# First adaptive-norm modulation summed on TensorE instead of VectorE, with the first norm and its first transposes issued in the same stage

## The reference, cut to what matters

```python
cond = jax.nn.silu(c)                                     # c: 2048 values
mod = (cond @ ada_w[l] + ada_b[l])[:, None, :]            # ada_w: 2048 x 12288
sh1, sc1, g1, sh2, sc2, g2 = jnp.split(mod, 6, axis=-1)
h = rms_norm(x, norm_mix[l]) * (1.0 + sc1) + sh1
x = x + g1 * hybrid_mixer(h, w_in[l], ...)                # begins with h @ w_in
```

## Time and profile before

| | |
|---|---|
| time, median of 3 executions | 4131.59 us (4130.81 to 4135.14) |
| profiled execution, its own time | 4132.34 us |
| its span in the trace | 4130.6 us |
| granted clock of TensorE, mean | 0.945 of full |
| busy: PE, DVE, ACT | 3661.5, 2459.1, 1249.8 us |
| end of the last DVE sum, start of the first matmul of `project_in` | 132.9 us, 160.45 us |

### The profile page before, as it was taken

One profiled execution on the slowest core, in us unless ns is written; L12 is line 12 of the kernel. 1 busy time (PEld: TensorE's weight loads), 2 busy tenths in 40 slices (PEclk: granted clock), 3 DMA queues, 4 the chain that ended last, 5 costly groups with the idle time before them and its releaser, 6 DMA issues. The chain is left out here.

```text
span 4130.6 us, 47822 instructions
## 1 busy us (share of the span) xinstructions
PE 3661.5 (89%) x19719; PEld 2918.5 (71%) x19719; DVE 2459.1 (60%) x3050; ACT 1249.8 (30%) x1316; POOL 253.3 (6%) x413
## 2 busy tenths in 40 slices
PE   2699868999999999999999799777978998799798
PEld 1575547799999999888888678376854775444576
DVE  7665658589777754555555454755445444694464
ACT  1223223334444444333333343212312101100233
POOL 1011101000100000000000000020000211000000
PEclk9999869999999999999999899798988999899899
DMA  7875327455766676766666452203643111443563
GB/s 268 305 261 188 117 78 296 151 204 196 260 247 251 248 255 213 251 237 242 245 244 236 159 219 91 87 6 124 228 139 133 32 37 57 133 152 117 182 251 133
DMA packets 246294, 750.73 MB, mean 182 GB/s; under 512 B 31264, under 2 KB 42612, under 8 KB 210368
## 3 DMA queue, kind: packets, MB, share of 16 engines
q1 hardware_dynamic: 217008, 645.44, 44.5%
q0 software_dynamic: 29072, 102.25, 7.1%
HBM read 692.29 MB, written 54.75 MB: 181 GB/s over the span
## 5 line engine op out<-in xcount | busy, mean ns | idle before, releaser
L2076 DVE TENSOR_TENSOR expert_w_low<-expert_w,expert_w_high 128x2048 fp32r<-128x2048 f32 x256 | 586.5, 2291 | 556.3 <-ACT expert_w_high L2368 555.8
L2368 ACT ACTIVATE expert_w_high<-expert_w 128x2048 fp32r<-128x2048 f32 x256 | 489.4, 1912 | 431.6 <-PE bank L2357 410.6
L289 DVE TENSOR_TENSOR weights_low<-weights,weights_high 128x1024 fp32r<-128x1024 f32 (+2 forms) x328 | 387.2, 1183 | 354.9 <-ACT weights_high L272 351.7
L2298 PE MATMUL bank<-h_high,expert_w_high 128*128 128x256 f32 x2048 | 583.5, 285 | 9.2 <-DVE expert_w_low L2076 8.2
L2299 PE MATMUL bank<-h_low,expert_w_high 128*128 128x256 f32 x2048 | 580.2, 283 | 0.0
L2300 PE MATMUL bank<-h_high,expert_w_low 128*128 128x256 f32 x2048 | 580.2, 283 | 0.0
L272 ACT ACTIVATE weights_high<-weights 128x1024 fp32r<-128x1024 f32 (+2 forms) x328 | 335.9, 1026 | 559.2 <-PE bank L317 462.4
L2298 PEld LDWEIGHTS bank<-h_high,expert_w_high 128*128 128x128 f32 x2048 | 393.8, 192 | 10.1 <-DVE expert_w_low L2076 8.8
L2355 PE MATMUL bank<-expert_w_high,gated_acts_high 128*128 128x512 f32 x1024 | 398.3, 389 | 0.0
L2356 PE MATMUL bank<-expert_w_low,gated_acts_high 128*128 128x512 f32 x1024 | 398.3, 389 | 0.0
L2357 PE MATMUL bank<-expert_w_high,gated_acts_low 128*128 128x512 f32 x1024 | 398.3, 389 | 0.0
(11 more groups left out here) (661 smaller groups left out, 5694.6 us busy)
## 6 DMA issues: line engine op xcount, KB each, us to landing
expert_w<-in_peer_u_dram SPq DMA_DIRECT2D x128, 1024.0 KB, 5.9
expert_w<-in_peer_v_dram SPq DMA_DIRECT2D x128, 1024.0 KB, 4.9
weights<-in_w_in_dram SPq DMA_DIRECT2D x84, 1024.0 KB, 9.7
ada_ring<-in_ada_w_dram SPq DMA_DIRECT2D x64, 512.0 KB, 5.1
weights<-in_w_out_dram SPq DMA_DIRECT2D x32, 1024.0 KB, 13.6
s_gates_w<-in_w_in_dram SPq DMA_DIRECT2D x64, 512.0 KB, 3.4
s_in_w<-in_w_in_dram SPq DMA_DIRECT2D x48, 512.0 KB, 4.1
weights<-in_w_branch_dram SPq DMA_DIRECT2D x48, 512.0 KB, 5.8
```

The costliest lines, as they stand in the source:

```text
L289: dve.tensor_tensor(self.low[:, u % self.UNITS_HELD, :, 0:n], self.buf[b][:, k:k + self.UNIT, 0:n], self.high[:, u % self.UNITS_HELD, :, 0 ...
L2076: dve.tensor_tensor(wl[:, n % RING, :], w_sb[:, n % RING, :], wh[:, n % RING, :], ALU.subtract).then_inc(wl_ready, 1)
L2298: pe.matmul(o, uh[:, b, k, :], acts.h[:, k, :], start=(k == 0), stop=False)
L2368: act.activation(wh[:, n % RING, :], w_sb[:, n % RING, :], ACT.Copy).then_inc(wh_ready, 1)
```

## The change

The sum over `ada_w` moves from DVE to PE. `cond_spots` holds, for each block k and each of eight chunks j of 512 columns, a stationary operand of 128 rows by 8 columns that is zero but for column j, which is `cond[:, k]`. A matmul with it and half a piece as the moving operand adds chunk j's sums to row j of one PSUM bank; all 128 of them (16 blocks, 8 chunks) accumulate in the same bank of 8 x 512. DVE copies it, four small transposes make columns of it, and DVE adds the bias vector. The accumulator, its clearing (L431), the 64 additions of L459 and the 32 matmuls of L489 are gone.

DVE takes the vector columns and fills `cond_spots` before it builds the masks. PE makes the bias table after block 3 (`if k == KD // 4`). The first norm's `source` is now made ahead of the stage: ACT and DVE run `head_act` and `head_dve` in it, and PE runs `turn_first`, the first 16 transposes, after block 13. `headed = True` takes the heads out of `project_in`. SP's loop is written out. The core of the diff:

```diff
+        spots = m.sb(ctx, "cond_spots", [P, KD, SUMS, SUMS])
+        sums = m.sb(ctx, "mod_sums", [SUMS, CHUNK])
...
-                with sp.Fori(0, KD) as k:
+                for k in range(KD):
                     for b in range(4):
-                        sp.wait_ge(piece_used[b], k)
-                        sp.dma_start(ring[:, b, :], io["ada_w"][0, bass.ds(k * P, P), b * PIECE:(b + 1) * PIECE])\
+                        if k:
+                            sp.wait_ge(piece_used[b], k)
+                        sp.dma_start(ring[:, b, :], io["ada_w"][0, k * P:(k + 1) * P, b * PIECE:(b + 1) * PIECE])\
                           .then_inc(piece_loaded[b], 16)
...
+                V(dve.memset(spots[:, :, :, :], 0.0))
+                for g in range(3):
+                    bank = m.to_dve.get(dve)
+                    m.to_dve.free(dve.tensor_copy(st.vec.cols[:, g, :], bank[:, 0:P]))
+                dve.engine_nop()
+                dve.drain().then_inc(cols_ready, 1)
+                dve.wait_ge(cond_ready, 1)
+                dve.tensor_copy(view(spots[:, 0, 0, 0:1], [[SUMS * SUMS, KD], [SUMS + 1, SUMS]]),
+                                spread(cond[:, :], SUMS)).then_inc(spots_ready, 1)
...
                 bias_dve(dve, V)
-
-                dve.wait_ge(cond_ready, 1)
-                with dve.Fori(0, KD) as k:
-                    for b in range(4):
-                        dve.wait_ge(piece_loaded[b], 16 * (k + 1))
-                        part = acc[:, b * PIECE:(b + 1) * PIECE]
-                        dve.scalar_tensor_tensor(out=part, in0=ring[:, b, :], scalar=cond[:, bass.ds(k, 1)],
-                                                 in1=part, op0=ALU.mult, op1=ALU.add).then_inc(piece_used[b], 1)
-                        dve.wait_ge(piece_used[b], k + 1)
-                dve.drain().then_inc(acc_ready, 1)
+                source.head_dve(dve)
+
                 bank = m.to_dve.get(dve)
+                m.to_dve.free(dve.tensor_copy(sums[:, :], bank[0:SUMS, :]))
+                dve.drain().then_inc(sums_ready, 1)
...
                 bias_act(act)
+                source.head_act(act)
...
-                bias_pe(pe)
-
-                pe.wait_ge(acc_ready, 1)
-                pe.wait_ge(ones_ready, 1)
+                pe.wait_ge(spots_ready, 1)
+                total = m.to_dve.take(pe)
+                for k in range(KD):
+                    if k == KD // 4:
+                        bias_pe(pe)
+                    if k == KD - 2:
+
+                        m.to_act.take_all(pe)
+                        source.turn_first(pe)
+                    for b in range(4):
+                        pe.wait_ge(piece_loaded[b], 16 * (k + 1))
+                        for half in range(2):
+                            j = 2 * b + half
+                            mm = pe.matmul(total[0:SUMS, :], spots[:, k, j, :], ring[:, b, half * CHUNK:(half + 1) * CHUNK],
+                                           start=(k == 0 and j == 0), stop=(k == KD - 1 and j == SUMS - 1))
+                        if k < KD - 1:
+                            mm.then_inc(piece_used[b], 1)
+                m.to_dve.put(mm)
+                pe.wait_ge(sums_ready, 1)
                 bank = m.to_dve.take(pe)
-                for j in range(NM // P):
-                    mm = pe.matmul(bank[:, j:j + 1], acc[:, j * P:(j + 1) * P], ones[:, :], start=True, stop=True)
+                for q in range(CHUNK // P):
+                    mm = pe.transpose(bank[:, q * SUMS:(q + 1) * SUMS], sums[:, q * P:(q + 1) * P], st.ident[0:SUMS, 0:SUMS])
                 m.to_dve.put(mm)
```

More of the change, by code:

```diff
@@ L261, in split_high @@
         b, turn = self.chunk["act"] % 2, self.chunk["act"] // 2
-        if source:
+        if source and not source.headed:
             source.head_act(act)
@@ L363, in turn_to_columns, with stage_modulation @@
         ring.put(mm)
-def stage_modulation(nc, m, io, st):
+def stage_modulation(nc, m, io, st, source):
     NM = 2 * D
     PIECE = NM // 4
+    SUMS = NM // CHUNK
     with ExitStack() as ctx:
@@ L445, in _ @@
                     V(dve.tensor_tensor(st.level[:, lv, :], tmp[:, :], st.strict[:, :], ALU.mult))
-                for g in range(3):
-                    bank = m.to_dve.get(dve)
-                    m.to_dve.free(dve.tensor_copy(st.vec.cols[:, g, :], bank[:, 0:P]))
-                dve.engine_nop()
-                dve.drain().then_inc(cols_ready, 1)
-                bias_dve(dve, V)
-                dve.wait_ge(cond_ready, 1)
-                with dve.Fori(0, KD) as k:
-                    for b in range(4):
-                        dve.wait_ge(piece_loaded[b], 16 * (k + 1))
-                        part = acc[:, b * PIECE:(b + 1) * PIECE]
-                        dve.scalar_tensor_tensor(out=part, in0=ring[:, b, :], scalar=cond[:, bass.ds(k, 1)],
-                                                 in1=part, op0=ALU.mult, op1=ALU.add).then_inc(piece_used[b], 1)
-                        dve.wait_ge(piece_used[b], k + 1)
-                dve.drain().then_inc(acc_ready, 1)
-                bank = m.to_dve.get(dve)
-                m.to_dve.free(dve.tensor_tensor(st.mod_cols[:, 0:NM // P], bank[:, 0:NM // P],
-                                                st.vec.col("ada_b", 0, NM // P), ALU.add))
+                bias_dve(dve, V)
+                source.head_dve(dve)
+                bank = m.to_dve.get(dve)
+                m.to_dve.free(dve.tensor_copy(sums[:, :], bank[0:SUMS, :]))
+                dve.drain().then_inc(sums_ready, 1)
+                bank = m.to_dve.get(dve)
+                parts = CHUNK // P
+                m.to_dve.free(dve.tensor_tensor(view(st.mod_cols[:, 0:1], [[1, parts], [parts, SUMS]]),
+                                                view(bank[:, 0:1], [[SUMS, parts], [1, SUMS]]),
+                                                view(st.vec.col("ada_b", 0), [[1, parts], [parts, SUMS]]), ALU.add))
                 dve.drain().then_inc(mod_cols_ready, 1)
@@ L610 @@
     TURNED_AHEAD = 4
+    headed = False
     def __init__(self, m, st, name, dst, kt, k0=0):
@@ L646, in columns @@
         if unit == max(self.unit0 - 1, 0):
-            self.head_pe(pe)
-            while self.n_turn < min(self.TURNED_AHEAD, self.pairs):
-                self.turn_next(pe)
+            self.turn_first(pe)
         if p >= 0:
@@ L656, in head_pe, with turn_first @@
         pass
+    def turn_first(self, pe):
+        self.head_pe(pe)
+        while self.n_turn < min(self.TURNED_AHEAD, self.pairs):
+            self.turn_next(pe)
     def turn_next(self, pe):
@@ L972, in project_in @@
         m.weights.split_memory(ctx)
-        source = NormedColumns(m, ctx, st, "norm1", st.x, D, acts, lambda j: st.gain1[:, j:j + 1],
-                               lambda j: st.mod_cols[:, j:j + 1], proj[:, :, 0:D], lambda tt: proj[:, tt, 0:D],
-                               x_sem=(m.sem("x_loaded"), 32), keep=st.whole)
         mod = ModulationParts(m, io, st, ctx, "mod_mid", (2,))
@@ L3851, in whole_program @@
             m.weights.memory(c1)
-            stage_modulation(nc, m, io, st)
             proj = m.sb(c1, "projection_rows", [P, TT, N_IN])
+            source = NormedColumns(m, c1, st, "norm1", st.x, D, None, lambda j: st.gain1[:, j:j + 1],
+                                   lambda j: st.mod_cols[:, j:j + 1], proj[:, :, 0:D], lambda tt: proj[:, tt, 0:D],
+                                   x_sem=(m.sem("x_loaded"), 32), keep=st.whole)
+            source.headed = True
+            stage_modulation(nc, m, io, st, source)
             with ExitStack() as c2:
                 h1 = Split(m, c2, "h1", KD)
-                project_in(nc, m, io, st, h1, proj)
+                source.dst = h1
+                project_in(nc, m, io, st, h1, proj, source)
             rows = m.sb(c1, "mixer_rows", [P, TT, HALF])
```

8 lines of the change are left out of this document (3 added, 5 removed).

## The result

| | before | changed |
|---|---|---|
| time, median of 20 runs each | 4134.06 us (4128.98 to 4141.03) | 4141.96 us (4132.44 to 4147.11) |
| ratio to before, 95% interval | | 1.0017 (1.0010 to 1.0024) |
| profiled execution, own time and span | 4132.34, 4130.6 us | 4144.02, 4142.3 us |
| first matmul of the projection in it | 160.45 us | 166.22 us |
| busy: PE, DVE | 3661.5, 2459.1 us | 3765.0, 2375.3 us |

The change costs 7 us (4 to 10 by the interval), inside the 0.2% that the prediction called no change. DVE is relieved of 84 us and PE is given 103 more, and neither number is the 7.

What follows compares the result with a forecast made beforehand. The ring's round paced the old sums, PE the new. 14.2 + 110.1 + 2 + 5 + 23 + 2.4 + 2.5 + 5.5 = 164.7 us at the first matmul against 160.45, so 4136 us; range 4122 to 4150.

Steps and rivals of the forecast that it cites:

- Rival A: The forecast itself for the whole kernel: 4127 to 4149 us, its low end with the bias table at the higher clock; chance 0.66.
- Steps 3 and 4: During the sums on PE: 2 us for transfers under them; 5 us (2 to 8) for two cold starts of PE's clock.
- Step 1: Start of the stage: the first piece lands and PE's sums start at 14.2 us, bounds 12 to 16.
- Step 2: The sums on PE: 256 records at the higher clock, 0.43 us each, 110.1 us; at the lower clock 220.
- Rival B: PE never gets the higher clock in this stage: 4246 us; a partial fall costs 20 to 60 us more; chance 0.18.
- Step 5: Bias table in PE's line between two runs of sums: first five us at the higher clock, rest low, 23 us.
- rival C: Bias table also at the higher clock, 13.8 us for 23, no second cold start: 4124 to 4125 us; chance 0.09.
- Steps 6 to 8: After the bias table, turns 2.4 us; after the sums, tail 2.5; from gain to the projection's first matmul, head 5.5.
- Step 9: Transfers after the stage: next loads shift by 24 to 28 us against 25 of slack; cost 0, up to 5 us.
- rival D: Late weights hold up the projection's first or second chunk by 5 to 10 us: 4141 to 4146 us; chance 0.07.
- one to one: From the projection's first matmul (160.45 us before) to the end: a shift there carries to the kernel's end in full.
- the ring's round: DVE's sums before: 1.285 us use plus 5.1 landing plus issue, 6.7, over four buffers is the 1.675 us per piece.

Runs made afterwards that it cites:

- experiment 7: The changed kernel with bias table operands of 128 rows and six buffers for the pieces: 4128.77 us, ratio to the kernel before 0.9985.
- experiment 9: Against the kernel before: DVE sums 48 of 64 pieces, PE 16; bias table spread between pieces with 128 rows, early norm, seven buffers: 4094.64 us, ratio 0.9909.
- experiment 3: The changed kernel with the first norm and its first turns back in the projection: 4148.18 us, ratio to the kernel before 1.004.
- experiment 2: The changed kernel with the bias table's two operands filled with zero rows from 33 to 128: 4130.0 us, ratio to the kernel before 0.9994.
- experiment 1: The changed kernel without the bias table's 16 matmuls (ACT fills the table from x, biases wrong): 4116.79 us, ratio to the kernel before 0.996.
- experiment 8: Against the kernel before: DVE sums 24 pieces, PE 40; six buffers, bias table operands of 128 rows, early norm: 4109.35 us, ratio 0.9941.
- Experiment 5: The kernel before with three, four, five or seven buffers, DVE's loop unrolled: 4156.32, 4136.77, 4118.62 and 4107.56 us (seven: ratio 0.9949).

## Why the prediction was right

Forecast: first matmul 4.3 us later, the time 4136 against 4131.59 (4.4 more). Measured: 5.8 at the first matmul, and 7 (4 to 10) by the ratio. The median of 4141.96 is 6 over the 4136: 2.5 of it because the kernel before reads 4134.06 over 20 executions, 1.5 at the first matmul, and the last 2 belong to no step. (Rival A's upper end adds up to 4150 and not 4149: 4.7, 2.5, 2 and 5 over 4136. Nothing hangs on it.) By its own steps:

| step | forecast | measured |
|---|---|---|
| 1 start | 14.2 | 15.43 |
| 2 sums, 256 records | 110.1 | 110.1 (0.430 each in experiment 7) |
| 3 transfers under them | 2 | 2.6 |
| 4 cold starts | 5 | 5.3 |
| 5 bias table | 23 | 23.0 |
| 6 turns | 2.4 | 1.9 |
| 7 tail | 2.5 | 1.8 |
| 8 head of the projection | 5.5 | 6.1 |
| first matmul | 164.7 | 166.22 |

The misses lie on both sides, and part of the nearness of the sum is that they cancel. Steps 3 and 4 are parted by the single records. The sums took 158.28 - 15.43 - 22.96 for the table - 1.9 for the turns = 118.0 us, 7.9 over the bare records. In the changed kernel six records of 1.01 to 1.06 us stand at the start, some 0.43 us lost on each, 2.5 in all; behind the table it is six and most of a seventh, 2.8. That leaves 2.6 for waits, of which the view shows 0.55 as gaps. The experiments agree: with 128 rows there is no second cold start, 114.5 us; with six buffers besides, no gap either, 112.0, and the 1.9 left over are a first cold start of only four full low records. So that start differs from run to run, and a difference of two runs can't give it to a few tenths.

- **Step 1** is the largest miss, 1.2 us. The start came within the bounds 12 to 16. The second half of x, issued at 6.7 us, landed 6.9 later, at 13.6, and the first piece 1.8 us behind it, more than the 1.26 a piece takes by itself: the transfers ran beside each other and not in order.
- **Step 2** was the large bet, 110 us either way. L1413 was the right neighbour: a form of 8 columns and 128 rows reached the higher level and kept it. Rival B would have shown 0.86 us a record; it is out. The Trainium skill's rule that a loop with long waits for DMA between its matmuls goes cold (TensorE: Matmul & The Clock Gate, "Loop structure matters more than you think") didn't come to bear: the waits were 2.6 us in 118, and the granted clock in the last stretch shown is 1.00. In experiment 9, where PE waited 1.3 to 3.6 us between many of its pieces, the clock did fall now and then: 0.87 in the stretch shown, and the last piece ran at 1.2 GHz.
- **Step 5** was right to 0.1 us, by a guess of five us high and the rest low, for which no row stood: ten records ran high here, thirteen in experiment 3, where the same table took 21.99. So the 0.1 is luck. What the prediction left open is why the table doesn't hold the higher level, and experiment 2 shows it: the 33 rows. The rule on the same page of the Trainium skill that sustained work lifts the clock ("What's actually happening") fails for this form, which was busy 23.03 us without a gap and fell from 589 to 1057 ns. With 128 rows it holds, and rival C, which hung on that rule, comes true as an experiment: 12.9 us less at the first matmul where 11.7 was worked out.
- **Steps 6 to 8**: the early norm is worth 4.6 us at the first matmul (experiment 3). The turns ran at the higher level, 1.97 for 3.65. From the gain on it took 6.1: ACT starts on the weights 0.3 after the gain, as forecast, and the chain from DVE's first low part to the first matmul took 4.8 us (161.44 to 166.22) where 4.2 was taken.
- **Step 9** was right in its cost, and wrong in part of its working. The first weights are requested 25.7 us later, but the second chunk's 32.0 and not 24 to 28, because the store of the bias table took longer to land. The slack of 25 us was used up, and ACT waited 5.1 us for them. This is what rival D feared, at ACT; on PE it cost next to nothing (the distance is 5.5 us at 422 us), so its price of 5 to 10 us is out.

What the profiled pair shows later is not settled. At 2344 us the distance is still 5.6. The start of L2612 at 3539 us is 9.8 later in the changed kernel, where its line is L2632 (3548.9 for 3539.1).

The other 4 us came in between, and the runs of either kernel differ among themselves by more. In experiment 1 it went by still more: its lead over the kernel before was 18.2 us at the first matmul, 24.5 at 2344 us and 18.1 at the end. The medians over many runs don't ask for a further cause: 7 with an interval from 4 holds the 5.8. Over the timed experiments the shift at the first matmul and that of the median agree within 6 us (against the kernel before, -22.7 and -25.5 with seven buffers, -9.7 and -4.2 in experiment 7, -29.0 and -23.7 in experiment 8, -41.9 and -37.7 in experiment 9), not better, so "one to one" is good to that.

The prediction also saw that the ring's round set the pace of before. Experiment 5 makes that a measured fact, and it shows what the change went past: DVE wasn't too slow for these sums, it was kept waiting. PE's 1.72 us per piece is no less than the 1.675 of the ring, so moving the work could win nothing in the sums and had to pay for the table; three more buffers, with the unrolled loop, won 25 us.

## What to carry to other kernels

Before work is moved to another engine, divide a buffer's round (use plus landing) by the number of buffers; if that is the pace seen, add a buffer first, since it costs no engine anything, only room (512 KB each here). Work that used to lie under another engine's stretch is not free to the engine that takes the stretch over: the bias table was hidden before and cost 24 us after. And where two engines draw on one ring, neither may be away longer than the buffers last.

## What the runs showed of the hardware

- An f32 matmul of 512 columns on 33 rows cost more than the same on 128: 1057 ns a record against 592, since only the second kept TensorE at 2.4 GHz. The 33-row form didn't only fail to raise the clock: coming in at the higher level it lost it after ten records (thirteen in experiment 3), and the sums behind it started cold. Few columns did no such harm: with 128 rows and 8 stationary columns the clock rose and stayed (0.430 us a record over 160 records in experiment 7).
- POOL's small selects (33 elements, one per partition) were held up by single operations of DVE. By themselves they take 0.18 us. In experiment 9, where DVE sums pieces beside them, in order of time:

```profile
15.37 0.18 POOL L1251 TENSOR_SCALAR_AFFINE_SELECT bucket_hi<-bucket_hi 33x1 f32<-33x1 f32 x1
15.44 1.28 DVE L481 SCALAR_TENSOR_TENSOR ada_acc<-ada_ring,cond,ada_acc 128x1024 f32<-128x1024 f32 x1 [5.88 <-DMA ada_ring<-in_ada_w_dram]
15.69 1.07 POOL L1251 TENSOR_SCALAR_AFFINE_SELECT bucket_lo<-bucket_lo 33x1 f32<-33x1 f32 x1
...
16.90 2.60 DVE L481 SCALAR_TENSOR_TENSOR ada_acc<-ada_ring,cond,ada_acc 128x1024 f32<-128x1024 f32 x2 [0.18 <-DMA ada_ring<-in_ada_w_dram]
16.91 0.18 POOL L1251 TENSOR_SCALAR_AFFINE_SELECT bucket_hi<-bucket_hi 33x1 f32<-33x1 f32 x1
17.23 1.00 POOL L1251 TENSOR_SCALAR_AFFINE_SELECT bucket_lo<-bucket_lo 33x1 f32<-33x1 f32 x1
```

  The select that starts at 15.69 ends at 16.76, 0.04 us after DVE's sum. Over experiments 8 and 9, 22 selects started inside one of DVE's operations of 1.28 us (the sums, and the scaling of the rows); 20 of them ended 0.04 us after it, however late they had started, and the other two began within 0.01 us of its start. All others there took 0.18 us, and so did seven beside the clearing of the accumulator in the kernel before (178 to 180 ns) and those beside an ACT that was busy for 9.90 of 10 us (experiment 1, 179 ns in the mean). Beside DVE's operations of 0.29 us on the masks a few took up to 0.31 (changed kernel). So it isn't DVE's load that counts but which operation is under way. In experiment 9 this put POOL's end from 24.2 to 37.5 us, of which the table felt only the last 1.4.
- The landing of a 512 KB piece rose less than the depth of the ring: 4.6, 5.2, 5.6 and 5.5 us with three, four, five and seven buffers, while the rate rose to 402 GB/s. In experiment 9, also with seven but at 411 GB/s, it was 6.9.
